# Rows of 64 tokens' two choices stored side by side and loaded 128 at a time, a twelfth expert slot, and another order in attention's front and end

## The reference, cut to what matters

```python
h = einsum('bld,de->ble', x, w_in)               # rq rk rv rg mq mk mv ga gb
o_r = group_norm(retention(rq, rk, rv)) * gn_g * silu(rg)       # 4 heads of 128
o_m = moba(mq, mk, mv)                                          # 8 heads of 64, block sparse
merged = sigmoid(ga + b) * (o_r @ w_br_ret) + sigmoid(gb + b) * (o_m @ w_br_moba)
x1 = layer_norm(ALPHA * x + merged @ w_out)
g_idx = argmax(x1 @ w_rg + b_rg)                                # 4 groups
e_val, e_idx = top_k(expert logits of that group, 2)            # 8 experts per group
hid = silu(x1 @ w_eg[e]) * (x1 @ w_eu[e])                       # 32 experts, hidden 128
out = sum over the two chosen e of weight_e * (hid @ w_ed[e])
y = layer_norm(ALPHA * x1 + out)
```

## Time and profile before

| | |
|---|---|
| three runs | 691.24, 693.68, 694.03 us; median 693.68 |
| profiled execution | 689.35 us, span of the instructions 687.5 us |
| mean granted clock | 0.949 |
| busy over the span | PE 610.0 us (89%), DVE 309.6 (45%), ACT 143.4 (21%), POOL 75.4 (11%) |
| moved by DMA | 124.43 MB, 181 GB/s on the mean |
| chain that ended last, by engine | PE 75%, DVE 8%, DMA 8%, issue 3%, ACT 3%, SP's queue 2% |

### The profile page before, as it was taken

The page is one execution under the profiler, slowest core; times in us unless marked ns, Lnnn a source line. Parts: engine busy times, 40 slices in busy tenths (PEclk is TensorE's granted clock), DMA queues, the critical chain, the costliest instruction groups (busy, mean ns, idle before and its releaser), DMA issues.

```text
span 687.5 us, 10970 instructions
## 1 busy us (share of the span) xinstructions
PE 610.0 (89%) x4390; PEld 502.6 (73%) x4390; DVE 309.6 (45%) x602; ACT 143.4 (21%) x290; POOL 75.4 (11%) x78
## 2 busy tenths in 40 slices
PE   3999999999998798799999999999933999999863
PEld 2999999999975564699999998788732555554410
DVE  6344343444337568734445544464575122222126
ACT  0111011030155255310001112120111232322202
POOL 0101400021052000000000000000003122221114
PEclk9999999999998999989999999999955999999977
DMA  9425322136307435022333312595078799999195
GB/s 355 160 75 173 117 62 92 61 92 210 115 21 219 119 118 185 32 62 92 123 138 128 106 59 92 208 415 209 33 279 315 276 409 417 414 415 384 69 211 178
DMA packets 45977, 124.43 MB, mean 181 GB/s; under 512 B 6289, under 2 KB 19729, under 8 KB 41714
## 3 DMA queue, kind: packets, MB, share of 16 engines
q1 hardware_dynamic: 39888, 112.23, 46.1%
q0 software_dynamic: 4752, 8.93, 3.5%
q10 hardware_dynamic: 1298, 2.73, 1.0%
HBM read 114.62 MB, written 17.43 MB: 192 GB/s over the span
## 4 chain that ended last, share of the span: by engine, by line
PE 75%; DVE 8%; DMA 8%; issue 3%; ACT 3%; SPq 2%; POOLq 0%; DVEq 0%; ACTq 0%
PE ps L709 13%; PE ps L707 13%; PE ps L708 13%; PE ps L1035 6%; PE ps L702 6%; DMA scratch<-experts 3%; PE ps L1050 3%; DMA arena<-token_rows 3%; PE ps L926 2%; PE ps L983 2%; PE ps L928 2%; PE ps L927 2%; PE ps L985 2%; PE ps L984 2%; PE ps L769 1%
## 5 line engine op out<-in xcount | busy, mean ns | idle before, releaser
L707 PE MATMUL ps<-xa_hi,w_hi 128*128 128x272 f32 x704 | 205.8, 292 | 11.4 <-DVE xa_lo L1441 11.4
L709 PE MATMUL ps<-xa_hi,w_lo 128*128 128x272 f32 x704 | 204.4, 290 | 0.0
L708 PE MATMUL ps<-xa_lo,w_hi 128*128 128x272 f32 x704 | 203.8, 290 | 0.0
L707 PEld LDWEIGHTS ps<-xa_hi,w_hi 128*128 128x128 f32 x704 | 133.7, 190 | 12.7 <-issue 10.0
L708 PEld LDWEIGHTS ps<-xa_lo,w_hi 128*128 128x128 f32 x704 | 133.9, 190 | 0.0
L709 PEld LDWEIGHTS ps<-xa_hi,w_lo 128*128 128x128 f32 x704 | 133.6, 190 | 0.0
L1432 DVE CAST w_hi<-w_ring 128x1024 fp32r<-128x1024 f32 x52 | 37.9, 729 | 114.3 <-PE ps L709 85.0
L1434 DVE TENSOR_TENSOR w_lo<-w_ring,w_hi 128x1024 fp32r<-128x1024 f32 x52 | 65.7, 1263 | 1.8
L1035 PE MATMUL ps<-arena,work 128*64 128x256 f32 x384 | 49.7, 394 | 2.9 <-ACT work L1269 2.2
L1374 POOL DMA_INDIRECT work<-x_rows,idx_i x13 | 13.3, 1027 | 343.3 <-DVE idx_i L1814 312.9
L1035 PEld LDWEIGHTS ps<-arena,work 128*64 128x64 f32 x384 | 29.8, 141 | 17.6 <-ACT work L1269 2.9
(11 more groups left out here) (263 smaller groups left out, 874.6 us busy)
## 6 DMA issues: line engine op xcount, KB each, us to landing
w_ring<-w_tiles SPq DMA_DIRECT2D x52, 512.0 KB, 3.5
arena<-experts SPq DMA_DIRECT2D x24, 1024.0 KB, 13.9
arena<-experts SPq DMA_DIRECT2D x24, 512.0 KB, 16.9
arena<-kT_pool SPq DMA_DIRECT2D x16, 256.0 KB, 3.1
out<-arena SPq DMA_DIRECT2D x4, 1024.0 KB, 5.4
arena<-v_pool SPq DMA_DIRECT2D x16, 256.0 KB, 2.9
arena<-token_rows SPq DMA_DIRECT2D x8, 512.0 KB, 11.3
cst<-experts SPq DMA_DIRECT2D x3, 1024.0 KB, 23.0
```

The lines of the kernel that those rows point to most:

```text
L707: mm(out, w_hi[b][:, w], x_hi[:, k_x, cols], start=start, stop=False)
L708: mm(out, w_hi[b][:, w], x_lo[:, k_x, cols], start=False, stop=False)
L709: return mm(out, w_lo[b][:, w], x_hi[:, k_x, cols], start=False, stop=stop)
```

## The change

- Result rows. Token t's rows of choice c went to row c * 544 + t. Now each 64 tokens have 128 rows: first their first choices, then their second (row 128 * (t / 64) + 64 * c + t mod 64). At the end one load fills 128 partitions with 128 consecutive rows; before, one load filled 64 partitions with two rows each. Number of loads and bytes are as before. The row numbers take more DVE instructions, behind the release of the token numbers.
- Twelve slots. The twelfth expert buffer is `arena[:, 0:EW]`, which holds the rows of tokens 0 to 383. These are therefore loaded again from DRAM after pair 11 (`s_x`, now also waited for by PE at the end). Experts 7 and 11 are loaded only when the first gather has landed. The last norm's parameters are loaded after the experts instead of before.
- Attention's front. RQ is projected before MQ; DVE evacuates it and multiplies by the decay in the same instructions, and POOL's multiplications go. The decay table is wider, so the constants are 295 KB more.
- Attention's end. For gate tiles 0 and 1 ACT casts the high part, DVE only subtracts; tile 1 gets a buffer of its own (`w_buf`). The 16 row scalings go from DVE to ACT. The five row transposes (X) now stand between gate tile 0 and the products of pair 3, in free banks (`x_bank`), and gate tile 1 directly behind.
- Router. 49 matmuls of the identity with itself, whose result nothing reads (`stay_active`), stand in three groups on PE: before the ranks, before the slot tables, before the first transposes.

```diff
-SLOTS = 11
+SLOTS = 12
-ROWS = 2 * T + COLS
+ROW0 = 2 * NP + CAP + NS
+ROWS = ROW0 + COLS
-MK, RK, RV, RG, MV, MQ, RQ = range(7)
+MK, RK, RV, RG, MV, RQ, MQ = range(7)
-                        w_ring[:, :, :].rearrange("p a n -> p (a n)")[:, 0:EW])[s - 8]
+                        w_ring[:, :, :].rearrange("p a n -> p (a n)")[:, 0:EW], arena[:, 0:EW])[s - 8]
...
-                 + [("N", ("rows",))] + turned(3) + O("sel", 1) + [("G", (0,))] + O("pv", 3))
+                 + turned(3) + [("N", ("rows",)), ("W", (1,))] + O("sel", 1) + [("G", (0,))]
+                 + [("X", (t,)) for t in range(TT)] + O("pv", 3) + [("G", (1,))])
...
@@ SP
-            for s in range(3, 8):
+            for s in range(3, 7):
                 load_parts(s, experts_d[s])
-            sp.dma_start(ln_g, ln2_g.partition_broadcast(P)).then_inc(s_ln2, 16)
-            sp.dma_start(ln_b, ln2_b.partition_broadcast(P)).then_inc(s_ln2, 16)
+            sp.wait_ge(s_gx[0], 16)
+            sp.wait_ge(s_x1t, TT)
+            sp.wait_ge(s_x1s, 16 * TT)
+            for s in (7, 11):
+                load_parts(s, experts_d[s])
...
             refill_down(10)
+            sp.wait_ge(s_dn, 12)
+            sp.dma_start(x_tm[:, 0:3], x1_d[0:3 * P].rearrange("(t p) n -> p t n", p=P)).then_inc(s_x, 16)
+            sp.dma_start(ln_g, ln2_g.partition_broadcast(P)).then_inc(s_ln2, 16)
+            sp.dma_start(ln_b, ln2_b.partition_broadcast(P)).then_inc(s_ln2, 16)
...
             for t in range(TT):
-                for c in range(2):
-                    rows = rows_d[c * T + t * P:c * T + t * P + r]
+                for g in range(2):
                     if t < 4:
-                        sp.dma_start(picked[c * CAP:(c + 1) * CAP, t], rows.rearrange("(g p) n -> p g n", g=2)
-                                     ).then_inc(s_yg[t], 16)
+                        at = (2 * t + g) * P
+                        sp.dma_start(picked[:, t, g], rows_d[at:at + P]).then_inc(s_yg[t], 16)
...
@@ PE
+            def stay_active(n):
+                for _ in range(n):
+                    mm(ps[:, 3, 0:P], ident, ident, start=True, stop=True)
+            stay_active(17)
             pe.wait_ge(s_msk, 1)
...
+            stay_active(17)
             for n in range(2 * TT):
...
             m.then_inc(s_ohu, 1)
+            stay_active(15)
...
+            pe.wait_ge(s_x, 48)
             for t in range(4):
...
@@ ACT
+            def high_parts(m):
+                act.wait_ge(s_o, max(done("reto", 3), done("cross", 1)))
+                act.wait_ge(s_s, used(("samp", 1)))
+                act.wait_ge(s_w[m % 4], 16 * (8 + m // 4))
+                A(w_hi[w_buf(m)][:], w_ring[:, m % 4, :], ACT.Identity).then_inc(s_hi, 1)
+            def scaled_rows():
+                act.wait_ge(s_gnm, 1)
+                for t in range(4):
+                    for h in range(RH):
+                        o = rk_t[:, t, h * P:(h + 1) * P]
+                        n = 4 * h + t
+                        m = A(o, o, ACT.Identity, scale=gstd[:, n:n + 1], bias=gmv[:, n, 0:1])
+                    m.then_inc(s_nr, 1)
...
@@ POOL
-            for h in range(RH):
-                q = fm[:, 4 * FM_OF[RQ] + h, 0:NP].rearrange("p (c n) -> p c n", c=4)
-                m = pv.tensor_tensor(q, q, C("qdec").rearrange("p (h n) -> p h n", h=RH)[:, h:h + 1, :]
-                                     .to_broadcast([P, 4, P]), ALU.mult)
-            m.then_inc(s_qd, 1)
...
@@ DVE, in the projections of RQ
+                    v.tensor_tensor(q[:, 0:HALF], ps[:, b, 0:HALF], decay, ALU.mult)
+                    v.tensor_tensor(q[:, HALF:NP], ps[:, b + 1, 0:NP - HALF], decay[:, skip:skip + NP - HALF], ALU.mult)
+                    v.tensor_copy(q[:, NP:T], ps[:, b + 1, NP - HALF:HALF]).then_inc(s_pev, 1)
...
@@ DVE, row step of the group norm
-                    for h in range(RH):
-                        o = rk_t[:, t, h * P:(h + 1) * P]
-                        n = 4 * h + t
-                        m = v.tensor_scalar(o, o, gmv[:, n, 0:1], gstd[:, n:n + 1], ALU.subtract, ALU.mult)
-                    ch.link(m)
+                    dve.wait_ge(s_nr, t + 1)
                     v.tensor_tensor(rg_t[:, t, :], rg_t[:, t, :], rk_t[:, t, :], ALU.mult).then_inc(s_gn, 1)
```

More of the change, by code:

```diff
@@ L98, in constants @@
     put("cmask", P, np.stack([np.where(p[None, :] >= p[:, None], ks * np.exp(-g * (p[:, None] + 1)), 0) for g in lg], 1))
[L99 removed]
+    put("qdec", P, np.tile(np.stack([np.exp(g * (np.arange(HALF) % P + 1)) for g in lg], 0)[None], (P, 1, 1)))
     put("kdec", P, np.tile(np.stack([ks * np.exp(g * (P - 1 - p)) for g in lg], 1)[:, :, None], (1, 1, 4)))
@@ L203, in hybrid_step @@
         oh_lo, oh_hi = under(0, [("slot_in_pair", [P, 2 * TT, P]), ("pair_of_slot", [P, 2 * TT, EVEN])])
+        earlier, = under(6912, [("earlier", [P, 2 * P])])
         sel_t, = under(4096, [("selected", [P, TT, NE])])
@@ L884, in gate, with turn_rows @@
                 b = 0 if kind == "a" else 2
-                project_split(m % 2, b, 0, xa_hi, xa_lo)
-                project_split(m % 2, b + 1, 1, xa_hi, xa_lo).then_inc(s_tile, 1)
+                project_split(w_buf(m), b, 0, xa_hi, xa_lo)
+                project_split(w_buf(m), b + 1, 1, xa_hi, xa_lo).then_inc(s_tile, 1)
+            def turn_rows(t):
+                pe.wait_ge(s_gn, t + 1)
+                if t < 2:
+                    pe.wait_ge(s_tu, nT)
+                elif t < 4:
+                    pe.wait_ge(s_su, nS)
+                else:
+                    pe.wait_ge(s_ou, done("sel", 1))
+                b = x_bank(t)
+                if t < 4:
+                    for c in range(4):
+                        m = tr(ps[:, b, c * P:(c + 1) * P], rg_t[:, t, c * P:(c + 1) * P], P)
+                else:
+                    m = tr(ps[:, b, 0:P], xs, P)
+                m.then_inc(s_ot, 1)
             for kind, jb in ORDER:
@@ L1205, in gate_values @@
                   bias=bm[:, 8 * u + n:8 * u + n + 1]).then_inc(s_cgs, 1)
-            for t in range(TT):
-                act.wait_ge(s_ot, t + 1)
-                b = t_bank(nT + t)
-                cols = slice(t * P, (t + 1) * P) if t < 4 else slice(NP, T)
-                r = P if t < 4 else NS
-                A(o_r[:, R_HI:R_HI + 4, cols], ps[:, b, 0:4 * r].rearrange("p (c n) -> p c n", c=4), ACT.Identity
-                  ).then_inc(s_otc, 1)
-                if t == 0:
-                    gate_values(0)
-            A(earlier[:], cst[:, CO["before"][0]:CO["before"][0] + 2 * P], ACT.Identity).then_inc(s_tri, 1)
+            gate_values(0)
             def wo_high(k):
@@ L1256, in _ @@
                 m.then_inc(s_x1c, 1)
+            A(earlier[:], cst[:, CO["before"][0]:CO["before"][0] + 2 * P], ACT.Identity).then_inc(s_tri, 1)
             act.wait_ge(s_gexp_i, 1)
```

140 lines of the change are left out of this document (80 added, 60 removed).

## The result

The changed kernel takes 672.58 us in the median of four runs (669.23 to 673.75); the kernel before took 692.46 (690.04 to 694.03) beside it. The ratio is 0.971, with an interval of 0.966 to 0.976: faster, and 0.9 us from the forecast of 671.7. The profiled execution took 672.23 us with a span of 670.4, 17.1 us less than the span before. PE is busy for 92% of it instead of 89%, the mean granted clock is 0.973 instead of 0.949, and 126.31 MB are moved instead of 124.43.

The account below looks back on a forecast made before the run. PE bounds it at full clock from 300 to 430 us; waits, half clock and DMA bind elsewhere. Terms -1.5 - 5.3 - 8.2 - 7.0 = -22.0 us from the median 693.68 give 671.7 us, range 664 to 682.

Parts of the forecast that it names:

- front and attention's end: Attention's two terms: -1.5 us at its front and -5.3 us at its end.
- router and experts: From router to the last expert pair: gather, matmuls of the identity and twelfth slot together end pair 15 8.2 us sooner.
- result rows: At the kernel's end: loads filling 128 partitions bring rows sooner, tiles 2.97 instead of 4.71 us apart; -7.0 us.
- the wait before the last pair: Sign at the last expert pair: PE has no wait over 1 us before it.
- first gather: In the router: engines free because experts 7 and 11 are held back; -1.5 us, with a gather under 4.5 us as sign.
- first pair: Sign at the first expert pair: it runs in under 4.5 us on PE, at a raised clock.
- Front: Attention's front: without POOL's multiplications DVE's scaling of probabilities is shorter; -1.5 us, bounds 0 and 2.35.
- Attention's end: Around gate tiles 0 and 1: PE's waits and half-clock work go, against 1.7 us of delay by ACT; -5.3 us.
- fourth rival: Attention's end stays: ACT's seventeen instructions ahead of the row blocks become the wait; 677.0 us, chance 0.06.
- Fillers: Router: matmuls of the identity raise PE's clock for ranks, transposes and first pair; -2.8 us, bounds 0 and -3.4.
- second rival: Router: matmuls of the identity miss, the clock falls before the gather, first pair slow again; +2.8, 674.5 us, chance 0.12.
- Twelve slots: Expert stage: pair 15 starts at 630.3 us, 2.7 gained less 0.3 of waiting, and runs 1.5 us shorter.

Follow-up runs that it names:

- again: The changed kernel with no edit, run and profiled a second time: 672.81 us, ratio 0.974 to the kernel before.
- experiment 4: The changed kernel with the decay of RQ on POOL again, between its two groups of masks, DVE only copying RQ: 675.64 us, ratio 0.978.
- experiment 3: The changed kernel with both halves of gate tile 0's split on DVE alone, as in the kernel before: 666.70 us, ratio 0.966.
- experiment 7: The changed kernel with no expert held back, so experts 7 and 11 wait for no gather: 674.76 us, ratio 0.975.
- experiment 2: The changed kernel without the 49 matmuls of the identity: 673.18 us, ratio 0.975.
- experiment 12: Changed kernel, gate tile 0 split on DVE before pair 2's products, only expert 11 held, 22 last identity matmuls, tile 3's sums first and repeated once: 662.44 us.
- experiment 8: The changed kernel with eleven expert slots and no reloaded rows: 675.38 us, ratio 0.977.
- experiment 6: The changed kernel with only expert 11 held back for the first gather, expert 7 following experts 3 to 6 at once: 669.32 us, ratio 0.967.
- experiment 1: The changed kernel with the result rows where they were, two loads of 64 partitions a token tile: 681.57 us, ratio 0.986.

## Why the prediction was right or wrong

| term, us | forecast | first profile | again |
|---|---|---|---|
| start | 0 | +1.55 | -0.34 |
| front and attention's end | -6.8 | -5.86 | -3.97 |
| router and experts | -8.2 | -5.61 | -5.57 |
| result rows | -7.0 | -7.19 | -8.72 |
| sum | -22.0 | -17.1 | -18.6 |

The sum on the profile was too large by 3 to 5 us. The medians differ by 19.9 (692.46 less 672.58), so the sum of 22.0 was 2.1 too large there, and the base, 693.68, 1.2 too high against the runs beside the result: the two errors make the 0.9. The range held the time and the total was right, but that it came so near is in part luck: the front gave 2.3 us more than forecast and the end of attention 3.5 to 3.8 less, and the experts 2.6 less. Of the signs that the prediction named for being right, the wait before the last pair failed (2.15 us, again 1.85), the first gather (4.61 and 4.25) and the first pair (3.67 and 5.21) each held in one of the two profiles, and the others held.

- *Front: mechanism right, size off.* Forecast 1.5, at most 2.35; measured 3.8 (experiment 4). All 2.35 came back, since the masks that start earlier don't slow the first inversion, and the transposes that had run at half clock behind the wait, 1.5 us, were left out of the bounds.
- *Attention's end: a step failed.* The prediction saw that tile 0's low part would wait for ACT and priced it at 1.7 us of delay. It took the half-clock transposes and the slow gate tile as gone with the old waits. But the 1.7 us are a pause of PE, and the clock fell behind that one: the slow stretch moved from gate tile 1 to the transposes and gate tile 0. From the sample products to the first branch product the end gained 1.8 us in the first profile and 1.5 in the second (44.33 less 42.56 and 42.88), not 5.3; with the split on DVE it gains 5.5 (experiment 3). That the second profile shows only -3.97 in the table is for the most part the clock ahead of `w_out`, of which the prediction says nothing. The fourth rival is the nearest in size, with a wrong cause: ACT's 16 scalings (6.25 us, 0.39 each) are not what PE waits for; in experiment 3, where gate tile 0 runs at full clock, they and what follows cost PE two waits of 0.52 and 0.94 us.
- *First gather: right, half the size.* 4.61 us, on empty engines, against 3.9 forecast. Beside six experts' loads it costs more than the rows of before showed: 7.27 us (experiment 7).
- *Fillers: right on PE, worth nothing at the end.* The prediction had PE's path and the loads level at the last pair (630.0 and 629.8 us) and counted PE's 2.8 us in full. The loads came later than that (below), so they alone set the end, and the first pair's 3.67 us instead of 5.58 is covered (experiment 2); where the loads have slack it counts (experiment 12). Whether it is 3.67 differs between executions of one kernel (here 3.67, again 5.21), as the second rival feared. The Trainium skill (TensorE: Matmul & The Clock Gate, section What's actually happening) has the hardware look at activity on a schedule of its own, and these two numbers of one kernel agree with it, without showing it.
- *Twelve slots: mechanism right, the loads mis-sized.* The slot is worth about 2.3 us (experiment 8), and the last pair behind its wait ran 3.67 us instead of 5.36, as forecast. But the loads took 105.5 us from the gather's landing (522.62) to the last pair (628.08) instead of 102.8, and PE waits 2.15 us there instead of 0.3. That the engines stand idle between the fourth expert and the gather (0.06 to 0.09 share) was read as good for the gather alone; that one more expert fits there, and takes PE's wait away, was not seen (experiment 6).
- *Result rows: right,* in mechanism and size (experiment 1): first rows 4.79 us after issue where 4.8 were forecast, then DVE's 2.97 a tile. The one slow tile that was allowed for came in the first profile and not in the second.

Which pause lets the clock fall stays open. In the six profiles with 15 calls where PE then waited 0.21 to 1.36 us for the gather, the first pair took 3.67 us; in the four where it waited 2.81 to 5.98, 5.15 to 6.60. With 22 calls it was 3.67 without a wait and 6.63 behind one of 1.64. But the same pause of 1.30 us ahead of pair 3's scores brought the clock down in seven profiles and not in six, so the length alone doesn't tell, and how many matmuls bridge the wait in every execution isn't known.

## What to carry to other kernels

Before adding up gains in a stage, say which resource sets its end: what another engine wins there is worth nothing until that resource has slack, and then the next wait (here reloaded rows) is the price. A pause on TensorE that a moved instruction creates is to be priced with the work behind it at half clock: 3.7 to 4.0 us here for a pause longer by 1.6. Two profiles of one kernel can differ by 2 us in a stage that no edit touched, so compare between marks that enclose only the edit. Loads into SBUF should fill 128 partitions; where they fill 64, look at GB/s beside the share of busy engines.

## What was not expected of the hardware

- Loads for partitions 0 to 63 and 64 to 127 in turn, queued behind each other, moved 215 to 217 GB/s at a share of 1.02; loads of 128 partitions, of the same bytes each, 418.
- The clock rose between 3.8 and 9.6 us after PE's first matmul, in 14 executions whose first tile is the same; the first score comes up to 2 us later for it.
- A gather of 128 token rows took 4.10 to 4.61 us where it had the DMA engines to itself or nearly so and the chain shows it, 7.27 on full ones.
- The clock fell behind a pause of PE of 2.29 or 2.30 us in nine profiles of nine, behind one of 2.05 to 2.15 us in five of nine, and behind one of 1.30 us in seven of thirteen.
